# 96 instead of 64 tokens by gathered expert rows, and GpSimd forms 14 low parts

## The reference

```python
q = (xb @ w_q).reshape(p, PEER_HEADS, 2, PEER_DK_HALF)
sc = jnp.einsum('phcd,hcnd->phcn', q, sub_keys)
top_s, top_i = lax.top_k(sc, PEER_TOPK)
...
g = jax.nn.softmax(best_s, axis=-1)
u_sel = expert_u[idx]
act = jax.nn.gelu(jnp.einsum('phkd,pd->phk', u_sel, xb), approximate=False)
coef = g * act
return jnp.einsum('phk,phkd->pd', coef, expert_v[idx])
```

## Time and profile before

| | us |
|---|---|
| median of 3 runs | 2380.35 |
| profiled execution | 2381.73 |
| its span | 2380.4 |
| PE busy | 2313.4 (97%) |
| DVE busy | 1578.9 (66%) |
| POOL busy | 951.0 (40%) |
| ACT busy | 856.4 (36%) |

### The profile page before, as it was taken

One profiled execution on the slowest core, in us unless ns is written; L12 is line 12 of the kernel. 1 busy time (PEld: TensorE's weight loads), 2 busy tenths in 40 slices (PEclk: granted clock), 3 DMA queues, 4 the chain that ended last, 5 costly groups with the idle time before them and its releaser, 6 DMA issues.

```text
span 2380.4 us, 29901 instructions
## 1 busy us (share of the span) xinstructions
PE 2313.4 (97%) x11272; PEld 2025.2 (85%) x11272; DVE 1578.9 (66%) x3014; ACT 856.4 (36%) x1335; POOL 951.0 (40%) x602
## 2 busy tenths in 40 slices
PE   6999999999899999999999999999999989999998
PEld 3777889999789999999999999998887778888887
DVE  6774699889996553588777777764856556434333
ACT  4433443333334333333333333353345534322221
POOL 1444208788888770033333433343332331111100
PEclk9999999999999999999999999999999999999999
DMA  7658746666667676579888888842424252333332
GB/s 289 195 148 251 211 138 170 162 153 160 163 150 188 169 182 206 196 301 343 322 321 330 315 349 298 300 132 86 130 67 116 70 188 89 97 97 98 102 98 76
DMA packets 199798, 443.60 MB, mean 186 GB/s; under 512 B 49180, under 2 KB 108700, under 8 KB 195104
## 3 DMA queue, kind: packets, MB, share of 16 engines
q1 hardware_dynamic: 139960, 319.12, 41.1%
q0 software_dynamic: 59696, 122.58, 17.3%
HBM read 374.06 MB, written 65.21 MB: 185 GB/s over the span
## 4 chain that ended last, share of the span: by engine, by line
PE 68%; DVE 3%; ACT 1%; issue 0%; ACTq 0%
PE bank L558 18%; PE bank L559 18%; PE bank L562 18%; PE bank_stat L935 1%; PE bank_stat L936 1%; PE bank_stat L940 1%; PE bank_stat L558 1%; PE bank_stat L562 1%; PE bank_stat L559 1%; DVE hot_weight L2010 1%; PE bank L967 1%; PE bank L965 1%; PE bank L980 1%; PE bank L710 1%; DVE weights_lo L1643 0%; PE bank_stat L585 0%
## 5 line engine op out<-in xcount | busy, mean ns | idle before, releaser
L558 PE MATMUL bank<-h_lo,weights_hi 128*128 128x448 f32 (+1 forms) x2148 | 813.8, 379 | 8.5 <-DVE gates L2311 3.8
L559 PE MATMUL bank<-h_hi,weights_hi 128*128 128x448 f32 (+1 forms) x2148 | 809.7, 377 | 0.0
L1119 ACT ACTIVATE weights_hi<-weights_raw 128x1024 fp32r<-128x1024 f32 (+1 forms) x411 | 432.1, 1052 | 498.1 <-PE bank L562 364.0
L1643 DVE TENSOR_TENSOR weights_lo<-weights_raw,weights_hi 128x1024 fp32r<-128x1024 f32 x351 | 443.6, 1264 | 196.9 <-ACT weights_hi L1119 194.5
L2489 POOL DMA_INDIRECT expert_coefs<-square x256 | 443.0, 1730 | 155.4 <-issue 79.0
L562 PE MATMUL bank<-h_hi,weights_lo 128*128 128x448 f32 (+1 forms) x2148 | 499.5, 374 | 1.4 <-DVE weights_lo L1643 1.4
L558 PEld LDWEIGHTS bank<-h_lo,weights_hi 128*128 128x128 f32 x2148 | 408.9, 190 | 61.3 <-DVE gates L2311 3.9
L559 PEld LDWEIGHTS bank<-h_hi,weights_hi 128*128 128x128 f32 x2148 | 408.5, 190 | 49.9 <-issue 0.2
L562 PEld LDWEIGHTS bank<-h_hi,weights_lo 128*128 128x128 f32 x2148 | 403.0, 188 | 52.3 <-DVE weights_lo L1643 2.5
L2436 POOL TENSOR_TENSOR weights_lo<-weights_raw,weights_hi 128x1024 fp32r<-128x1024 f32 x60 | 147.6, 2465 | 223.5 <-ACT weights_hi L1119 223.4
L1330 ACT ACTIVATE hidden<-bank 128x448 f32<-128x448 f32 x128 | 69.9, 546 | 406.4 <-PE bank L562 406.4
(11 more groups left out here) (463 smaller groups left out, 3424.7 us busy)
## 6 DMA issues: line engine op xcount, KB each, us to landing
weights_raw<-in_expert_u SPq DMA_DIRECT2D x128, 512.0 KB, 3.8
weights_raw<-in_expert_v SPq DMA_DIRECT2D x128, 512.0 KB, 4.6
weight<-expert_coefs POOLq DMA_DIRECT2D x16, 1792.0 KB, 10.0
hidden_store<-hidden SPq DMA_DIRECT2D x28, 896.0 KB, 6.1
hidden<-hidden_store POOLq DMA_DIRECT2D x14, 1792.0 KB, 15.1
ada_raw<-in_w_ada SPq DMA_DIRECT2D x34, 512.0 KB, 6.1
expert_coefs<-zeros SPq DMA_DIRECT2D x32, 512.0 KB, 6.4
expert_coefs<-stage SPq DMA_DIRECT2D x12, 1024.0 KB, 5.8
```

Of the source, the lines that this page charges most:

```text
L558: M.matmul(bank[:, 0:width], hi[:, c:c + P], m_lo[k][:, 0:width], start=start and i == 0, stop=False)
L559: M.matmul(bank[:, 0:width], hi[:, c:c + P], m_hi[k][:, 0:width], start=False, stop=False)
L1119: S.activation(w_hi[n % SPLIT][:, 0:w], w_raw[n % RAW][:, 0:w], ACT.Copy).then_inc(*hi_done.inc(n))
L1643: V.tensor_tensor(w_lo[n % SPLIT][:, 0:w], w_raw[n % RAW][:, 0:w], w_hi[n % SPLIT][:, 0:w].bitcast(F32), ALU.subtract).then_inc(*lo_dve.in ...
```

## The change

PICKED goes from 64 to 96, so the dense products have 416 columns. The picked tokens stand in BATCHES = 3 batches of 32; four partitions serve a token, and there are 96 row steps for U and 96 for V, with an accumulator `own0` to `own2` for each batch. ScalarE writes the tokens once into `scaled`, and `copy_own` on SP copies them to the three `own` tiles by 12 DMAs. VectorE's table of places (`row_at`) and weights (`row_share`) is written by 24 small copies in place of 6 operations. There are ROWS = 5 row buffers; the fifth, `row_over`, lies over `position` and `turns` and is free once the rotation angles are made, so the 17 steps for these are moved to the U blocks of place 0. The row steps are spread over `SLOTS`: the last four U blocks of place 0 and places 0 to 14, some 12 a place. Tokens 256 to 415 need 40 quads instead of 48. GpSimd forms the low part of the last V block (k = 7) at places 1 to 14; in its instructions that stands behind the load of the seventh row of the place. In the diff below the allocation of tiles is left out but for the row buffers.

```diff
@@ -35,10 +35,13 @@
 QUADS = P // 4
-PICKED = 64
+PICKED = 96
+BATCH = 32
+BATCHES = PICKED // BATCH
 DT = T - PICKED
-ROWS = 4
+ROWS = 5
 SCATTERED = 2
+TABLE_STEPS = 17
 ROUTE_STEPS = HEADS + HEADS // 2 + 4 + 2
...
@@ -165,6 +168,7 @@
     | set(range(BLOCK_AT["w_branch_a", 1], BLOCK_AT["w_branch_b", 3] + 2))
+POOL_LOW |= {BLOCK_AT["expert_v", g * KD + KD - 1] for g in MIX_ORDER[1:-1]}
 POOL_LOW -= {BLOCK_AT["w_q", 1], BLOCK_AT["w_q", 2]}
...
@@ -338,11 +344,15 @@
         mixed = [(mixed_hi, mixed_lo), (h_hi, h_lo), (last_hi, last_lo)]
+        over = ExitStack()
+        row_over = sb("row_over", [P, D], F32, over)
+        over.close()
         position = sb("position", [P, T], I32, scope)
         turns = sb("turns", [P, T], F32, scope)
-        own_sum = sb("own_sum", [P, D], F32, scope)
+        own = [sb(f"own{b}", [P, D], F32, scope) for b in range(BATCHES)]
         rows = [sb(f"rows{i}", [P, D], F32, scope)[:] for i in range(2)] \
-            + [t[:].rearrange("p k t -> p (k t)") for t in (square, scaled)]
+            + [t[:].rearrange("p k t -> p (k t)") for t in (square, scaled)] + [row_over[:]]
+        own_tokens_x = scaled[:].rearrange("p k t -> p (k t)")
         scope.close()
...
@@ -468,9 +478,10 @@
 
+        SLOTS = [(0, "u", n) for n in range(HALF, GROUP)] + [(i, k) for i in range(N_GROUPS - 1) for k in range(KD)]
         ROW_STEPS = {}
         for q in range(2 * PICKED):
-            ROW_STEPS.setdefault(divmod(GROUP + q * (N_GROUPS - 2) * GROUP // (2 * PICKED), GROUP), []).append(q)
+            ROW_STEPS.setdefault(SLOTS[q * len(SLOTS) // (2 * PICKED)], []).append(q)
 
...
@@ -520,7 +531,7 @@
             n_quads = min(QUADS, (DT - tb * P) // 4)
-            room = min(QUADS, AHEAD * GROUP - 2 - first)
+            room = min(n_quads * TB // 2, QUADS, AHEAD * GROUP - 2 - first)
             for quad in range(n_quads):
...
@@ -834,7 +845,9 @@
                             M.wait_ge(*dve["row", 2 * PICKED - 1])
-                            ins = M.matmul(held_bank(k)[:, DT:T], own_sum[:, k * P:(k + 1) * P], fold[:], start=True, stop=True)
+                            for b in range(BATCHES):
+                                ins = M.matmul(held_bank(k)[:, DT + b * BATCH:DT + (b + 1) * BATCH], own[b][:, k * P:(k + 1) * P],
+                                               fold[:], start=True, stop=True)
                         ins.then_inc(*pe.inc(("v", g, k)))
...
@@ -1983,12 +1995,15 @@
                     V.wait_ge(*dve["routed", tb])
-                    for half, to in enumerate((slice(64, 128), slice(0, 64))):
-                        slots = slice(half * PICKED, (half + 1) * PICKED)
-                        V.tensor_copy(row_share[to, :], chosen[64:128, 2, slots]).then_inc(*dve.inc(("row_share", half)))
-                        chain(V.scalar_tensor_tensor(row_coef[to, :], chosen[64:128, 0, slots], float(N_KEYS), chosen[64:128, 1, slots],
-                                                     ALU.mult, ALU.add))
-                        chain(V.tensor_copy(row_at[to, :], row_coef[to, :]), ("row_at", half))
+                    chain(V.scalar_tensor_tensor(place_f, chosen[:, 0, :], float(N_KEYS), chosen[:, 1, :], ALU.mult, ALU.add))
+                    chain(V.tensor_copy(column_u, place_f), "row_numbers")
+                    for b in range(BATCHES):
+                        tokens = slice(P - PICKED + b * BATCH, P - PICKED + (b + 1) * BATCH)
+                        columns_of = slice(b * BATCH, (b + 1) * BATCH)
+                        for part in range(P // BATCH):
+                            to = slice(part * BATCH, (part + 1) * BATCH)
+                            V.tensor_copy(row_share[to, columns_of], chosen[tokens, 2, to]).then_inc(*dve.inc(("row_share", b, part)))
+                            V.tensor_copy(row_at[to, columns_of], column_u[tokens, to]).then_inc(*dve.inc(("row_at", b, part)))
                 yield
...
@@ -2018,12 +2033,14 @@
 
-            V.tensor_tensor(fold[:], const("ident")[:, 0:PICKED], const("ident")[:, PICKED:P], ALU.add).then_inc(*dve.inc("fold"))
             routers = [route_tokens(tb) for tb in range(TB)]
             for h in range(HEADS):
                 ada_tile(40 + h)
                 next(routers[0])
             ada_columns(40, 48, 0.0, "gate2")
+            chain(V.tensor_tensor(fold[:], const("ident")[:, 0:BATCH], const("ident")[:, BATCH:2 * BATCH], ALU.add))
+            chain(V.tensor_tensor(fold[:], fold[:], const("ident")[:, 2 * BATCH:3 * BATCH], ALU.add))
+            chain(V.tensor_tensor(fold[:], fold[:], const("ident")[:, 3 * BATCH:P], ALU.add), "fold")
             for j in range(AHEAD * GROUP):
...
@@ -2081,22 +2098,23 @@
 
-                kind, s = divmod(q, PICKED)
+                kind, c = divmod(q, PICKED)
+                b, s = divmod(c, BATCH)
                 row = rows[q % ROWS]
                 if q == 0:
-                    V.wait_ge(*act["own_x", 1])
+                    V.wait_ge(*own_copied[BATCHES - 1, P // BATCH - 1])
                 if q == PICKED:
                     V.wait_ge(*act["row_gelu"])
                     chain(V.tensor_tensor(row_coef[:], row_coef[:], row_share[:], ALU.mult), "row_coef")
                 V.wait_ge(*rows_landed[q % ROWS][q])
                 if kind == 0:
-                    V.tensor_tensor_reduce(out=row, in0=row, in1=own_x[:], scale=1.0, scalar=0.0, op0=ALU.mult, op1=ALU.add,
-                                           accum_out=row_coef[:, s:s + 1]).then_inc(*dve.inc(("row", q)))
+                    V.tensor_tensor_reduce(out=row, in0=row, in1=own[b][:], scale=1.0, scalar=0.0, op0=ALU.mult, op1=ALU.add,
+                                           accum_out=row_coef[:, c:c + 1]).then_inc(*dve.inc(("row", q)))
                 elif s == 0:
-                    V.tensor_scalar(own_sum[:], row, row_coef[:, 0:1], None, ALU.mult).then_inc(*dve.inc(("row", q)))
+                    V.tensor_scalar(own[b][:], row, row_coef[:, c:c + 1], None, ALU.mult).then_inc(*dve.inc(("row", q)))
                 else:
                     V.wait_ge(*dve["row", q - 1])
-                    V.scalar_tensor_tensor(own_sum[:], row, row_coef[:, s:s + 1], own_sum[:], ALU.mult, ALU.add) \
+                    V.scalar_tensor_tensor(own[b][:], row, row_coef[:, c:c + 1], own[b][:], ALU.mult, ALU.add) \
                         .then_inc(*dve.inc(("row", q)))
...
@@ -2105,6 +2123,10 @@
                         split_lo(BLOCK_AT["expert_u", (g + 1) * GROUP + n] + 2)
+                        for _ in range(TABLE_STEPS // GROUP + 1):
+                            next(turning, None)
+                        for q in ROW_STEPS.get((i, "u", n), ()):
+                            row_step(q)
                 for k in range(KD):
...
@@ -2118,8 +2140,6 @@
                         dve.also(("held", k), ("x2", g, k))
-                    if i >= len(MIX_ORDER) - KEPT:
-                        next(turning, None)
                     for q in ROW_STEPS.get((i, k), ()):
...
@@ -2506,27 +2526,33 @@
             load_group(0)
+            G.dma_start(position[:], a["positions"]).then_inc(*position_landed.inc("position"))
             load_group(1)
-            G.dma_start(position[:], a["positions"]).then_inc(*position_landed.inc("position"))
 
             def load_rows(q):
 
-                kind, s = divmod(q, PICKED)
+                kind, c = divmod(q, PICKED)
                 if q >= ROWS:
                     G.wait_ge(*dve["row", q - ROWS])
+                elif rows[q] is rows[-1]:
+                    G.wait_ge(*dve["angle"])
                 G.indirect_dma_start(out=rows[q % ROWS], out_offset=None, in_=a[("rows_u", "rows_v")[kind]],
-                                     in_offset=bass.IndirectOffsetOnAxis(ap=row_at[:, s:s + 1], axis=0)) \
+                                     in_offset=bass.IndirectOffsetOnAxis(ap=row_at[:, c:c + 1], axis=0)) \
                     .then_inc(*rows_landed[q % ROWS].inc(q))
 
-            for half in range(2):
-                G.wait_ge(*dve["row_at", half])
-            load_group(2)
-            for i in range(1, len(MIX_ORDER)):
+            G.wait_ge(*dve["row_at", BATCHES - 1, P // BATCH - 1])
+            G.wait_ge(*own_copied[BATCHES - 1, P // BATCH - 1])
+            for n in range(GROUP):
+                for q in ROW_STEPS.get((0, "u", n), ()):
+                    load_rows(q)
+            for i in range(len(MIX_ORDER)):
                 steps_here = [q for k in range(KD) for q in ROW_STEPS.get((i, k), ())]
                 for n, q in enumerate(steps_here):
                     load_rows(q)
                     if n == ROWS - 1:
                         load_group(i + 2)
+                    if n == ROWS + 1 and i < len(MIX_ORDER) - 1:
+                        split_lo(BLOCK_AT["expert_v", MIX_ORDER[i] * KD + KD - 1] + 1)
                 if len(steps_here) < ROWS:
...
@@ -2648,6 +2674,15 @@
 
+            def copy_own():
+
+                Y.wait_ge(*dve["routed", TB - 1])
```

(6 more changed lines are left out.)

12 lines of the change are left out of this document (7 added, 5 removed).

## The result

The changed kernel takes 2458.12 us (median, 2453.18 to 2460.19, 4 runs) against 2381.11 before: a ratio of 1.0318 with a 95% interval of 1.0295 to 1.0341, 77 us slower. The forecast was 2413, with a range to 2450: the sign and the place were right, the size was not.

What follows compares the result with a forecast made beforehand. TensorE bounds nearly everywhere; in the changed mix a closed chain of waits sets the pace instead. Terms: 2381.7 - 27 - 5 + 62 + 1 - 2.6 + 3 = 2413 us, range 2384 to 2450.

Steps and rivals of the forecast that it cites:

- The columns: Dense products: 416 columns take 189.2 ns, so a block of 24 falls from 4.86 to 4.54 us.
- The mechanism: Mix: GpSimd's low-part wait closes a burst-to-burst chain of 43.5 us a pass, against TensorE's 36.3; +62 us.
- VectorE's lock-out: Mix: SBUF sharing with GpSimd's low part could cost VectorE up to 34 us; taken as nothing, VectorE mostly waiting then.
- The first rival: Mix: GpSimd's low part is hidden, a pass takes 37.2 or 36.3 us, the time is 2313 to 2326; chance 0.09.
- step 1: Mix chain, from burst issued to landing of row 5 right behind it: 17.2 us.
- 2, 3: to GpSimd's start: Mix chain: VectorE's row 5 and low part 5, tile 4's product, then ScalarE's high parts, the latter 1.6 us.
- 4: low part; issue and landing: Mix chain: GpSimd's low part 2.4 us, 0.3 to the next issue, row 7 to landing 4.8.
- 5, 6: to the next burst: Mix chain: VectorE's rows, low parts and mixes 12.3 us, then GpSimd's wake 0.3 and issue 1.67, to 43.5.
- its +3: Mix: five places with 13 rows, two with row 7 only in step 5, three with row 6 already in step 3.
- Place 0: First place: its 16 U and V blocks gain 5.1 us from fewer columns; the chain starts only in place 1.
- The clock is no term: Mix: a lower TensorE clock after its 7 us stops only eats time left over before the next wait.
- The rival of dearer links: Mix: VectorE's low part meeting GpSimd's and slower landings add 1.1 us each a pass, 26 in all, 2439; chance 0.12.

Runs made afterwards that it cites:

- wait_only: Changed kernel, but GpSimd only waits for block 7's high part at the same queue place and VectorE forms the low part: 2429.6 us, 1.0198.
- half_detour: Changed kernel with GpSimd's low part in only every second group, 7 of 14: 2411.6 us, 1.0115.
- lows_alone: Kernel before (64 tokens, 448 columns) with only GpSimd's low part of block 7 added in 14 groups: 2416.4 us, 1.0141.
- no_detour: Changed kernel without GpSimd's low part; VectorE forms block 7's low part in every group: 2366.6 us, 0.993.
- spread_detour: Changed kernel, GpSimd's low part kept, each burst of group loads cut into 8 pieces behind rows 4 to 11: 2413.2 us, 1.0129.
- block6: Changed kernel, but GpSimd forms the low part of block 6, not 7, at the same queue place; whole bursts: 2416.7 us, 1.0142.
- half_burst: Changed kernel with the second transfer (hidden_store, 1664 KB) of each burst from place 0 on left out: 2388.9 us, 1.0031.
- spread: Changed kernel without GpSimd's low part, each burst cut into 8 pieces, one behind each of rows 4 to 11: 2309.2 us, 0.9688.
- spread_table: Changed kernel without GpSimd's low part, bursts in 8 pieces, 6 table steps, not 3, beside each U block of place 0: 2310.5 us, 0.9698.
- spread_4: Changed kernel without GpSimd's low part, bursts in 8 pieces, four row buffers in place of five: 2317.7 us, 0.9727.
- spread_block6: Changed kernel with bursts in 8 pieces and GpSimd forming the low part of block 6, not 7, behind row 6: 2377.2 us, 0.9983.
- low_last: Changed kernel, but GpSimd's low part of block 7 stands behind the last row transfer of its place, not behind row 6: 2384.1 us, 1.0007.
- by_scalar: Changed kernel without GpSimd's low part, whole group loads issued by ScalarE on its own hardware queue: 2345.6 us, 0.9841.

## Why the prediction was wrong

**The columns: right.** The starts of nine products of 416 columns lie 1.51 us apart, 188.8 ns each for 189.2:

```profile
1041.39 0.35 PE L569 MATMUL bank<-mixed_lo,weights_hi 128*128 128x416 f32 x1
1042.90 0.35 PE L569 MATMUL bank<-mixed_lo,weights_hi 128*128 128x416 f32 x1
```

The U blocks end near 913, as said (block 120 leaves its bank at 913.76), and gain 34.8 by the first V product for 29.6. From 540 the routing stage gave 0.7 and did not lose 3, and the first 48 blocks gave 14 for 12.

**The mechanism: right in its order, too simple as a sum.** Every link came in the order given, in all thirteen passes behind a burst, and wait_only, half_detour and lows_alone met the numbers worked out from it. no_detour ended 0.6 us above a range that already used a measured landing; by the prediction's own number for a pass without the detour (37.2 us, 2313 to 2326) it is 40 us slower, by the same link and by place 0. Where one link was cut away and the others left, the sum did not hold: spread_detour 2413 for 2311 to 2350, block6 2417 for 2350 to 2385. VectorE's lock-out cost little: in ten of the thirteen passes nothing of VectorE ran beside GpSimd's low part. The first rival, a hidden detour, would have needed row 7 earlier; it came at 1118.81, 7 us late.

**The links: step 1 was mis-sized.** From 996.73 to 1547.22 there are 12 passes, 45.87 us each, and not 43.75. By link, mean of the 12:

| link | forecast | measured |
|---|---|---|
| 1: burst to the row behind it | 17.2 | 18.65 |
| 2, 3: to GpSimd's start | 4.5 | 4.8 |
| 4: low part; issue and landing | 2.4; 5.1 | 2.65; 4.6 |
| 5, 6: to the next burst | 14.3 | 15.1 |

Link 1 is 17 of the missing 25 us here; the low part is 3, the last links 10, and the landing of row 7 gave 6 back. In three passes (places 2, 7 and 12) VectorE needs the second row behind the burst too before GpSimd can start, 19.2 to 20.7 us behind it; this is what makes the 4.5 a 4.8, and the prediction had it in its +3. (The 18.95 us of the expectations count this second row.)

Link 1 failed in two ways. I took the middle of three landings (18.05 from the burst); the twelve bursts of the kernel before behind which VectorE stood give 18.6. And I took 0.8 off for 256 KB fewer. The row did not come sooner: in 18.9 us behind a burst the engines move, first before (1213.11), then after (1088.78),

```profile
DMA packets 1255, 7.25 MB, mean 384 GB/s; under 512 B 128, under 2 KB 128, under 8 KB 997
q0 software_dynamic: 683, 5.14, 68.4%
q1 hardware_dynamic: 570, 2.09, 29.4%
```

```profile
DMA packets 1396, 7.44 MB, mean 394 GB/s; under 512 B 158, under 2 KB 158, under 8 KB 1139
q0 software_dynamic: 819, 5.33, 69.9%
q1 hardware_dynamic: 576, 2.10, 27.8%
```

384 and 394 GB/s: they are full in both, and the bytes that the burst no longer has go to other transfers. A whole transfer less, as in half_burst, does show. Together the two are 1.3 to 1.4 of the 1.45 us.

**Place 0 was left out.** I let the chain begin at place 1, and place 0 had nothing but its gain in columns. The loop now starts with place 0, and its first burst goes there:

```profile
956.50 0.58 POOL L2522 DMA_DIRECT2D weight<-expert_coefs  x1
```

```profile
947.67 1.23 DVE L2111 CUSTOM_DVE_ANT_0 row_over<-row_over,own 128x1024 f32<-128x1024 f32 x1 [5.46 <-DMA row_over<-in_rows_u,row_at]
...
975.16 1.23 DVE L2111 CUSTOM_DVE_ANT_0 square<-square,own 128x1024 f32<-128x1024 f32 x1 [5.11 <-DMA square<-in_rows_u,row_at]
```

VectorE stands 5.46 us for the row in the fifth buffer, whose load waited for the last table step, and 5.11 behind the burst. So place 0 took 45.6 us and not 36.3: 9.3 of the missing 40. TensorE stood 5.8 of these (3.50 us at 950.06, 1.96 at 977.59, 0.38 at 992.51). The other 3.4 are the clock. Behind the first two stops TensorE was granted its lower level, 1.2 GHz, for part of the time:

```profile
950.00:956.00 6.00, 5.87 (x21) 4.90 (x22) 5.97 (x9) 2.57 (x4) 2.75 (x3) 0.72 0.97 360
974.00:980.00 6.00, 4.04 (x16) 3.58 (x15) 4.83 (x7) 1.82 (x3) 1.68 (x1) 0.82 1.02 396
980.00:986.00 6.00, 6.00 (x31) 5.94 (x29) 6.00 (x11) 1.50 (x2) 3.32 (x2) 0.90 0.85 311
```

What lacks to 1.00 in these three stretches of 6 us is 3.4 us. The prediction's "The clock is no term" held for the passes, whose links do not wait for TensorE, and not for place 0, where TensorE sets the end. With the burst in pieces place 0 still takes 42.2 (spread); where the wait for the table is gone as well (spread_table, spread_4) it is 36.2.

**Start and end.** The first burst of the chain goes 7.0 us into place 1 for 4, and from the last burst to the last group there are 83.7 us for 78. That is 8.7 together: the same dear link once more, and a stop of 3.08 us at 1623.49. Against all this stand 5 us that the U blocks gave more than forecast.

**The rival of dearer links** (2439) had the sign of the error and too little of it: landings one us later and a VectorE low part that meets GpSimd's. The landings came 1.4 later. Only two of the 12 passes had the latter (3.40 and 4.49 us in place of 2.39, and there it was GpSimd's that grew; in the first a VectorE product of a tile grew too, 2.77 for 0.59).

**What the chain did not say.** Cutting link 1 away did not free the detour. ScalarE's high part has three releasers (VectorE's mixed tile before it in its order, the raw weights, TensorE's buffer); I followed the one that came last and took the other two for early. With VectorE's wait gone (spread_detour) GpSimd still waits 12.93 us where it was 17.49; for the block before 12.01 and, with pieces, 8.60. What is left can be counted at VectorE, from the first product of place 1 to that of the last group. It works 31 to 33 us a group in every kernel with 96 tokens, and stands for rows 13.8 (after), 11.9 (wait_only), 11.8 (spread_detour), 10.3 (block6), 7.5 (spread_block6), 6.9 (no_detour) and 1.7 (spread), where TensorE's 36.2 takes over. This is a count and not a cause. Why the detour costs more with pieces (104 us) than with whole bursts (91.5) is not shown.

## What to carry to other kernels

A wait put into an in-order queue costs what stands behind it: ask who waits for that, and where the awaited value comes from at that moment, along all its releasers, not only the last. Here that wait decided whether 96 tokens lose or gain. Large transfers on the queue that also brings small urgent ones should be cut up between them: this was worth 57 us without the wait and 45 with it, and another queue for them only 21. For a recurring link take the mean over all its occurrences, and don't take a few per cent of its bytes off while the engines behind it are full.

## What the runs showed of the hardware

- The DMA engines moved 398 GB/s for 182 us at a share of 1.01 (spread, 1018 to 1200). The 375 that I worked out from 315 at 0.84 was too low. TensorE stayed full meanwhile.
- In spread a row's transfer takes 5.2 to 14.3 us from issue to landing (median 10.3), longer than in no_detour (median 8.0), and VectorE hardly stands: what matters is that no row takes 19.
- GpSimd's operation held a VectorE row step at 3.93 us for 1.22, and GpSimd's own took 3.40, 4.49 and 4.47 for 2.39 in three places of the kernel after. In low_last VectorE is the one held each time, by 2.0 to 2.7 us.
- Rows on another queue than the burst (by_scalar) land 18.1 us behind it on average, for 19.1 on the same queue.
- TensorE's granted clock in 1018 to 1563 was 0.92 with its stops of some 7 us a group, 0.95 in wait_only, 0.97 in no_detour and 0.99 in spread. The passes of the kernel after are accounted for without it; in place 0 it took 3.4 us.
